# Latent attention heads: the squares for the norms of q and k move from ACT, tile by tile, to POOL, half of the tokens at once

## The chip, the cores and the metric

The kernel runs on one core of a Trainium2 chip. Its engines are PE (TensorE: matrix products and transposes), DVE (VectorE), ACT (ScalarE), POOL (GpSimd), and SP (SyncE), which issues the DMA transfers here. The metric is the device time of one execution in microseconds (us); lower is better.

## The reference, cut to what matters

Two decoder layers on 1024 tokens of width 1024. Layer 0 mixes tokens by stick-breaking attention, layer 1 by latent attention; each layer also has memory heads, an output projection and a SwiGLU. The change touches only this part of layer 1:

```
q  = (rms(c_q,  mla_q_norm)  @ w_q_up ).reshape(b, s, 12, 96)
kv = (rms(c_kv, mla_kv_norm) @ w_kv_up).reshape(b, s, 12, 64 + 64)
k  = concat(kv[..., :64], k_rope for every head)
v  = kv[..., 64:]
q, k = rms(q, g_qn), rms(k, g_kn)          # over the 96 columns of each head
q, k = rope on the last 32 columns of each
o = causal softmax attention(q, k, v)
```

The norms need the sum of squares of each token's 96 columns of q, and of the 64 columns of k of each head, to which the sum over the 32 shared columns (k_ss) is added.

## The kernel before

Every large product is made in three passes (high by high, high by low, low by high) of operands that are split into a rounded high half and the rest, the low half. `latent_heads` handles the 12 heads in 6 pairs. Per pair, `prepare` runs these steps on all engines, each engine taking its part of a step in its own queue:

- project n (n = 0 to 7, one for each tile of 128 tokens): PE makes q, k and v of two heads in PSUM bank 7; ACT copies them out to q32, k32 and v32 (the eviction) and squares q and k head by head, with the row sums as accumulator output. The next project waits for the eviction, the bank being only one.
- sum n (n = 0, 1: the half of the tokens): DVE adds k_ss. root n: ACT takes the square root, which needs another table of functions than the exponential. normalise n: DVE takes the reciprocal and multiplies q and k. rotate n: DVE and POOL share the rotary part; POOL first writes the rotated part of k.
- next weights: ACT rounds the weights of the pair after, POOL subtracts (lower_weights). values n: the split of v for head n, by ACT and then POOL (lower_values).
- turn n (n = 0 to 7): PE transposes 512 tokens of q or k of one head into bank 7, ACT writes the high half, scaled, DVE the low half (L2255). Turn n waits for the low half of turn n-1; turns 0 and 2 wait for the normalised and rotated halves.

The attention itself is the class `Attend`: four jobs for each pair (two heads, two halves of the queries, with 4 and 8 blocks of keys), 24 places in all. Its step kinds: S, scores of a tile by PE, and their row maximum by DVE (L934); P, the exponential by ACT (L909); I and R, the reciprocal of the row sum and the scaling of the row by DVE (L940, L946); T, transposes of a block of weights by PE (L885), then high half by ACT (L917) and low half by DVE (L951); V, the product with the values (PV, L894 and L896), which needs both halves; E, the end of a job, by ACT (L923) and DVE (L957). All jobs use one output bank, so the first V of a job waits for E of the job before. At place tau PE does T of tau, V of tau-1, then the scores that `plan` allows, then what `extras` lists for that place. Every engine walks the same list in order, so whatever stands in front in a queue delays the rest.

The first pair is prepared alone (the start-up, list PREPARE). Then a loop runs five rounds: the attention of pair g with the preparation of pair g+1 at the places that `extras` names. The last pair's attention runs with no preparation. POOL walks its own order: rotate 0, lower_weights, rotate 1, lower_values. SP stores outputs and loads the weights of the pair after next. Before the change these lines hold the places:

```
extras = {..., 4: ["project 4", "sum 0", "root 0"], 5: ["project 5", "normalise 0"], 6: ["project 6", "rotate 0"],
          7: ["project 7"], 8: ["next weights", "sum 1", "root 1"], 9: ["normalise 1"],
          10: ["rotate 1", "turn 0"], 11: ["used 1", "turn 1"], 12: ["turn 2"], 13: ["values 0", "turn 3"],
          14: ["turn 4"], 16: ["turn 5"], 18: ["turn 6"], 21: ["turn 7"]}
```

## Time and profile before

| | |
|---|---|
| median of 3 runs | 3078.08 us |
| lowest and highest | 3076.92 and 3081.86 us |
| span of the profiled execution, first to last instruction | 3078.6 us |
| mean granted TensorE clock over the span | 0.939 |

The profile gives the execution's span and no time of its own beside it; the span lies 0.5 us above the median. Busy shares are means over stages with different limits. The latent heads take the stretch from about 1765 to 2262 us: the start-up until about 1826, five rounds of some 75 us, and the last. A number in square brackets at the end of a timeline row is the time for which the engine stood idle before that instruction, with what released it.

### The profile page before, as it was taken

How to read it: one execution, taken by the hardware profiler on the slowest of the kernel's cores; microseconds unless marked ns; L12 is line 12 of the kernel's file. 1: busy time of each engine (PE TensorE's matmuls, PEld its weight loads, DVE VectorE, ACT ScalarE, POOL GpSimd, SP SyncE). 2: the span in 40 equal slices, each digit the busy share in tenths (PEclk: the TensorE clock that was granted, in tenths of full speed). 3: DMA queues.
4: the chain of work that ended last, by engine and by line, in shares of the span. 5: the costliest groups of instructions: out<-in, count | busy, mean ns of one | idle time of the engine just before them, and what ended most of it. 6: DMA issues, size and time to landing. Idle time of an engine off the chain costs nothing. (4 is left out here: it accounts for less than half of the span.)

```text
span 3078.6 us, 40579 instructions
## 1 busy us (share of the span) xinstructions
PE 2705.0 (88%) x13104; PEld 2209.8 (72%) x13104; DVE 1480.0 (48%) x2547; ACT 1295.7 (42%) x2794; POOL 1038.7 (34%) x722
## 2 busy tenths in 40 slices
PE   5679999878999998998668668888879899998999
PEld 4567777657788887887548657777757688887887
DVE  5636666744755553111562236666643755553111
ACT  4436566634333332222442246666633433332222
POOL 2035555530544443443102011111120544443443
PEclk9899999989999999999788879999989999999999
DMA  3021000041222223454102000000041222223454
GB/s 111 11 65 28 28 27 27 7 171 69 82 82 82 82 82 144 143 171 147 39 14 57 23 12 18 19 18 18 9 169 69 82 82 82 82 82 134 143 171 140
DMA packets 143097, 232.38 MB, mean 75 GB/s; under 512 B 17056, under 2 KB 93856, under 8 KB 143008
## 3 DMA queue, kind: packets, MB, share of 16 engines
q1 hardware_dynamic: 143008, 231.24, 22.7%
q8 instruction: 50, 0.82, 0.1%
q14 instruction: 39, 0.32, 0.0%
HBM read 182.98 MB, written 48.23 MB: 75 GB/s over the span
## 5 line engine op out<-in xcount | busy, mean ns | idle before, releaser
L1487 POOL TENSOR_TENSOR l0s_run_lo<-l0s_run,l0s_run_hi 128x512 fp32r<-128x512 f32 (+3 forms) x144 | 177.2, 1231 | 200.9 <-DVE l0s_run_hi L1653 200.9
L365 POOL TENSOR_TENSOR l0f_dn_lo<-l0f_dn_raw,l0f_dn_hi 128x1024 fp32r<-128x1024 f32 x44 | 106.0, 2411 | 138.9 <-ACT l0f_dn_hi L431 138.9
L365 POOL TENSOR_TENSOR l1f_dn_lo<-l1f_dn_raw,l1f_dn_hi 128x1024 fp32r<-128x1024 f32 x44 | 106.0, 2412 | 138.3 <-ACT l1f_dn_hi L431 138.3
L82 PE MATMUL banks<-l0f_dn_hi,l0f_a_hi 128*128 128x512 f32 x352 | 139.4, 396 | 8.9 <-issue 5.3
L82 PE MATMUL banks<-l1f_dn_hi,l1f_a_hi 128*128 128x512 f32 x352 | 138.6, 394 | 9.5 <-issue 5.3
L82 PE MATMUL banks<-l1f_T_hi,l1f_op_hi 128*128 128x512 f32 x352 | 139.3, 396 | 7.4 <-DVE l1f_T_lo L538 7.2
L82 PE MATMUL banks<-l0f_T_hi,l0f_op_hi 128*128 128x512 f32 x352 | 140.1, 398 | 6.1 <-DVE l0f_T_lo L538 5.9
L84 PE MATMUL banks<-l0f_T_hi,l0f_op_lo 128*128 128x512 f32 x352 | 139.0, 395 | 0.0
L83 PE MATMUL banks<-l0f_dn_lo,l0f_a_hi 128*128 128x512 f32 x352 | 138.9, 395 | 0.0
L84 PE MATMUL banks<-l0f_dn_hi,l0f_a_lo 128*128 128x512 f32 x352 | 138.8, 394 | 0.0
L84 PE MATMUL banks<-l1f_T_hi,l1f_op_lo 128*128 128x512 f32 x352 | 138.8, 394 | 0.0
L83 PE MATMUL banks<-l0f_T_lo,l0f_op_hi 128*128 128x512 f32 x352 | 138.8, 394 | 0.0
L83 PE MATMUL banks<-l1f_dn_lo,l1f_a_hi 128*128 128x512 f32 x352 | 138.6, 394 | 0.0
L84 PE MATMUL banks<-l1f_dn_hi,l1f_a_lo 128*128 128x512 f32 x352 | 138.6, 394 | 0.0
L83 PE MATMUL banks<-l1f_T_lo,l1f_op_hi 128*128 128x512 f32 x352 | 138.4, 393 | 0.0
L1643 DVE SCALAR_TENSOR_TENSOR l0s_run<-banks,l0s_soft 128x512 f32<-128x512 f32 (+3 forms) x144 | 80.2, 557 | 119.0 <-ACT l0s_soft L1545 117.6
L951 DVE TENSOR_TENSOR l1aa_pt_lo<-banks,l1aa_pt_hi 128x512 fp32r<-128x512 f32 (+2 forms) x144 | 79.3, 551 | 115.9 <-ACT l1aa_pt_hi L917 115.7
L592 DVE TENSOR_TENSOR l0f_a_lo<-l0f_a_raw,l0f_a_hi 128x512 fp32r<-128x512 f32 x44 | 33.2, 756 | 206.0 <-ACT l0f_a_hi L429 206.0
L592 DVE TENSOR_TENSOR l1f_a_lo<-l1f_a_raw,l1f_a_hi 128x512 fp32r<-128x512 f32 x44 | 33.2, 756 | 205.4 <-ACT l1f_a_hi L429 205.4
L82 PE MATMUL banks<-ht_hi,l0s_w_hi 128*128 128x512 f32 x288 | 119.4, 415 | 12.5 <-POOL l0s_w_lo L1477 12.5
L1516 ACT ACTIVATE l0s_soft<-banks 128x512 f32<-128x512 f32 (+3 forms) x144 | 71.0, 493 | 139.3 <-PE banks L1710 96.5
L360 POOL TENSOR_TENSOR l0f_hid<-l0f_c,l0f_gate 128x512 f32<-128x512 f32 x44 | 67.2, 1529 | 174.2 <-DVE l0f_c L553 174.2
(480 smaller groups left out, 8572.1 us busy)
## 6 DMA issues: line engine op xcount, KB each, us to landing
l0f_raw<-in_w_ffn_gu_dram SPq DMA_DIRECT2D x22, 1024.0 KB, 5.2
l0f_dn_raw<-in_w_ffn_down_dram SPq DMA_DIRECT2D x44, 512.0 KB, 3.9
l1f_raw<-in_w_ffn_gu_dram SPq DMA_DIRECT2D x22, 1024.0 KB, 5.1
l1f_dn_raw<-in_w_ffn_down_dram SPq DMA_DIRECT2D x44, 512.0 KB, 3.9
hidden_rows<-l0f_hid SPq DMA_DIRECT2D x22, 512.0 KB, 2.7
l0f_a_raw<-hidden_rows SPq DMA_DIRECT2D x44, 256.0 KB, 3.1
hidden_rows<-l1f_hid SPq DMA_DIRECT2D x22, 512.0 KB, 2.7
l1f_a_raw<-hidden_rows SPq DMA_DIRECT2D x44, 256.0 KB, 3.0
```

Source lines behind the costliest of these rows:

```text
L82: pe.matmul(out, l_hi, r_hi, start=first, stop=False, skip_group_check=True)
L83: pe.matmul(out, l_hi, r_lo, start=False, stop=False, skip_group_check=True)
L84: return pe.matmul(out, l_lo, r_hi, start=False, stop=last, skip_group_check=True)
L360: pool.tensor_tensor(hidden(q), cs[q][:], gate[q][:], ALU.mult).then_inc(hid_done, 1)
L365: pool.tensor_tensor(dn_lo[e][:], dn_raw[e][:], as_f32(dn_hi[e][:]), ALU.subtract).then_inc(dn_lo_done, 1)
L592: dve.tensor_tensor(a_lo[e][:], a_raw[e][:], as_f32(a_hi[e][:]), ALU.subtract).then_inc(a_lo_done, 1)
L951: dve.tensor_tensor(self.pt_lo[tau % 2][:, c0:HALF], self.t_ps[tau % 2][:, c0:HALF], as_f32(self.pt_hi[tau % 2][:, c0:HALF]), ALU.subtract ...
L1487: pool.tensor_tensor(run_lo[t % NR][:, f:HALF], run[t % NR][:, f:HALF], as_f32(run_hi[t % NR][:, f:HALF]), ALU.subtract).then_inc(run_spli ...
L1516: act.activation(s[:, f:HALF], psum[b % NZ][:, f:HALF], ACT.Abs).then_inc(abs_done, 1)
L1643: dve.scalar_tensor_tensor(r[:, f:HALF], psum[t % NZ][:, f:HALF], 0.0, soft[t % NA][:, f:HALF], ALU.max, ALU.add).then_inc(sp_done, 1)
```

## The change

ACT no longer squares in `project`. POOL gets a step squares(n, g) that multiplies all of q of half n by itself (128x768) into a buffer sq, waits until DVE has summed that, and does the same for k (128x512). DVE's sum n becomes two steps: sumq n sums q's squares; sumk n sums k's squares and adds k_ss. POOL's order becomes squares 0, rotate 0, squares 1, rotate 1, lower_weights, lower_values. sq lies over the buffers ra to rd of the rotation, which is why squares(1) waits for q_rot. In the loop, the sums, roots, normalisations and rotations stand one to three places later than before, turns 2 to 6 one place later (turn 4 from 14 to 15, turn 7 stays), and the scores of the next pair from place 13 on up to one place later.

```diff
--- before.py
+++ after.py
@@ -2030,8 +2030,9 @@
     wq = {n: mem(f"{tag}_wq_{n}", [P, NQ, QW], F32 if n == "raw" else F32R) for n in ("raw", "hi", "lo")}
     wk = {n: mem(f"{tag}_wk_{n}", [P, NK, KW], F32 if n == "raw" else F32R) for n in ("raw", "hi", "lo")}
     q32, k32 = mem(f"{tag}_q32", [P, G, QK]), mem(f"{tag}_k32", [P, G, QK])
-    junk = mem(f"{tag}_junk", [P, 2, QK + NOPE])
+    turned_at = mem.at
     ra, rb, rc, rd = (mem(f"{tag}_{n}", [P, G, H]) for n in ("ra", "rb", "rc", "rd"))
+    sq = Memory(nc, turned_at, mem.at)(f"{tag}_sq", [P, G // 2, QK])
     qt = {n: mem(f"{tag}_qt_{n}", [QK, 2, S], F32R) for n in ("hi", "lo")}
     kt = {n: mem(f"{tag}_kt_{n}", [QK, 2, S], F32R) for n in ("hi", "lo")}
     ss, std, rstd = (mem(f"{tag}_{n}", [P, 2, G]) for n in ("ss", "std", "rstd"))
@@ -2042,18 +2043,18 @@
 
     turns = [(a, h, half) for h in range(2) for half in range(2) for a in range(2)]
 
-    PREPARE = (["project 0", "project 1", "project 2", "project 3", "sum 0", "root 0", "normalise 0", "rotate 0",
-                "project 4", "project 5", "project 6", "project 7", "next weights", "sum 1", "root 1", "normalise 1",
+    PREPARE = (["project 0", "project 1", "project 2", "project 3", "sumq 0", "sumk 0", "root 0", "normalise 0", "rotate 0",
+                "project 4", "project 5", "project 6", "project 7", "next weights", "sumq 1", "sumk 1", "root 1", "normalise 1",
                 "rotate 1", "values 0"] + [f"turn {n}" for n in range(8)])
 
 
     extras = {0: ["values 1", "project 0"], 1: ["project 1"], 2: ["project 2"], 3: ["project 3"],
-              4: ["project 4", "sum 0", "root 0"], 5: ["project 5", "normalise 0"], 6: ["project 6", "rotate 0"],
-              7: ["project 7"], 8: ["next weights", "sum 1", "root 1"], 9: ["normalise 1"],
-              10: ["rotate 1", "turn 0"], 11: ["used 1", "turn 1"], 12: ["turn 2"], 13: ["values 0", "turn 3"],
-              14: ["turn 4"], 16: ["turn 5"], 18: ["turn 6"], 21: ["turn 7"]}
-
-    plan = [8, 9, 10, 11, 12, 13, 13, 14, 14, 15, 15, 16, 16, 16, 17, 18, 19, 20, 20, 21, 21, 22, 22, 23, 24]
+              4: ["project 4"], 5: ["project 5", "sumq 0"], 6: ["project 6", "sumk 0", "root 0"],
+              7: ["project 7", "normalise 0"], 8: ["next weights", "rotate 0"], 9: ["sumq 1"],
+              10: ["sumk 1", "root 1", "turn 0"], 11: ["used 1", "normalise 1", "rotate 1", "turn 1"],
+              13: ["values 0", "turn 2"], 14: ["turn 3"], 15: ["turn 4"], 17: ["turn 5"], 19: ["turn 6"], 21: ["turn 7"]}
+
+    plan = [8, 9, 10, 11, 12, 13, 13, 14, 14, 15, 15, 16, 16, 16, 16, 17, 18, 19, 20, 20, 21, 22, 22, 23, 24]
     OWN = ("values 1", "used 1")
     group = lambda n: slice(G // 2 * n, G // 2 * (n + 1))
     tiles = lambda n: slice(NS // 2 * n, NS // 2 * (n + 1))
@@ -2072,10 +2073,10 @@
                      lambda h, half, g: ot_dram[bass.ds(g * P + h * HD, HD), half * HALF:(half + 1) * HALF],
                      low, 4, psum["pair"], (6,), plan, extras)
         sem = lambda n: ctx.semaphore(f"{tag}_{n}")
-        (g_in, wq_in, wk_in, wq_hi, wk_hi, wq_lo, wk_lo, made, evicted, squared, v_hi, v_split, sums, root, inverse,
+        (g_in, wq_in, wk_in, wq_hi, wk_hi, wq_lo, wk_lo, made, evicted, squared, v_hi, v_split, sums, q_sums, k_sums, root, inverse,
          q_norm, k_norm, k_rope_done, rot_dve, rot_pool, q_rot, turned, t_hi, t_split, ones, scaled) = (
             sem(n) for n in ("g_in", "wq_in", "wk_in", "wq_hi", "wk_hi", "wq_lo", "wk_lo", "made", "evicted", "squared", "v_hi",
-                             "v_split", "sums", "root", "inverse", "q_norm", "k_norm", "k_rope_done",
+                             "v_split", "sums", "q_sums", "k_sums", "root", "inverse", "q_norm", "k_norm", "k_rope_done",
                              "rot_dve", "rot_pool", "q_rot", "turned", "t_hi", "t_split", "ones", "scaled"))
         block = ctx.enter_context(nc.Block())
         bank = psum[7]
@@ -2092,7 +2093,7 @@
                 sp.dma_start(wk["raw"][:], k_rows[:, :, bass.ds(g * KW, KW)]).then_inc(wk_in, 16)
 
             at_.begin(sp)
-            for s in (made, evicted, squared, v_split, turned, t_split):
+            for s in (made, evicted, v_split, turned, t_split):
                 sp.sem_inc(s, 1)
             load(0)
             sp.wait_ge(ones, 1)
@@ -2126,6 +2127,16 @@
                     pool.wait_ge(hi, g + 1)
                     pool.tensor_tensor(w["lo"][:], w["raw"][:], as_f32(w["hi"][:]), ALU.subtract).then_inc(lo, 1)
 
+            def squares(n, g, first=False):
+                e = 2 * g + n
+                if not first:
+                    pool.wait_ge(q_rot, 2 * e)
+                pool.wait_ge(evicted, 1 + NS * g + NS // 2 * (n + 1))
+                pool.tensor_tensor(sq[:], q32[:, group(n), :], q32[:, group(n), :], ALU.mult).then_inc(squared, 1)
+                pool.wait_ge(q_sums, e + 1)
+                pool.tensor_tensor(sq[:, :, 0:NOPE], k32[:, group(n), 0:NOPE], k32[:, group(n), 0:NOPE],
+                                   ALU.mult).then_inc(squared, 1)
+
             def rotate(n, g):
                 e, x1n, x2n = 2 * g + n, x1[:, tiles(n)], x2[:, tiles(n)]
                 pool.wait_ge(inverse, e + 1)
@@ -2140,14 +2151,16 @@
                 pool.wait_ge(rot_dve, 2 * e + 2)
                 pool.tensor_tensor(x2n, four(rc, n), four(rd, n), ALU.add).then_inc(q_rot, 1)
 
-            def prepare(g):
+            def prepare(g, first=False):
+                squares(0, g, first)
                 rotate(0, g)
+                squares(1, g)
+                rotate(1, g)
                 lower_weights(g + 1)
-                rotate(1, g)
                 lower_values(0, 2 * g)
 
             lower_weights(0)
-            prepare(0)
+            prepare(0, True)
             with pool.Fori(0, PAIRS - 1) as g:
                 lower_values(1, 2 * g + 1)
                 prepare(g + 1)
@@ -2177,13 +2190,6 @@
                     act.activation(q32[:, two, :], bank[:, 0:QW].rearrange("p (g d) -> p g d", d=QK), ACT.Copy)
                     act.activation(k32[:, two, 0:NOPE], kv[:, :, 0:NOPE], ACT.Copy)
                     act.activation(v32[:, two, :], kv[:, :, NOPE:], ACT.Copy).then_inc(evicted, 1)
-                    act.wait_ge(evicted, 1 + NS * g + n + 1)
-                    act.wait_ge(squared, 1 + NS * g + n)
-                    for h in range(2):
-                        one = slice(2 * n + h, 2 * n + h + 1)
-                        act.activation(junk[:, h, 0:QK], q32[:, 2 * n + h, :], ACT.Square, accum_out=ss[:, 0, one])
-                        last = act.activation(junk[:, h, QK:], k32[:, 2 * n + h, 0:NOPE], ACT.Square, accum_out=ss[:, 1, one])
-                    last.then_inc(squared, 1)
                 elif what == "root":
                     act.wait_ge(sums, 2 * g + n + 1)
                     act.activation(std[:, :, group(n)], ss[:, :, group(n)], ACT.Sqrt, bias=k["eps"][:, 0:1],
@@ -2227,8 +2233,13 @@
 
                 what, n = step.split()[0], int(step[-1]) if step[-1].isdigit() else 0
                 e = 2 * g + n
-                if what == "sum":
-                    dve.wait_ge(squared, 1 + NS * g + NS // 2 * (n + 1))
+                if what == "sumq":
+                    dve.wait_ge(squared, 2 * e + 1)
+                    dve.tensor_reduce(ss[:, 0, group(n)], sq[:], AX, ALU.add).then_inc(q_sums, 1)
+                elif what == "sumk":
+                    dve.wait_ge(squared, 2 * e + 2)
+                    dve.tensor_reduce(ss[:, 1, group(n)], sq[:, :, 0:NOPE], AX, ALU.add).then_inc(k_sums, 1)
+                    dve.wait_ge(k_sums, e + 1)
                     ks = ss[:, 1, group(n)].rearrange("p (t h) -> p t h", h=2)
                     dve.tensor_tensor(ks, ks, k_ss[:, tiles(n)].unsqueeze(2).broadcast_to([P, NS // 2, 2]),
                                       ALU.add).then_inc(sums, 1)
```

## Rows read from the trace of the kernel before

**Rows 1.** page, part 1: busy us, share of the span, instructions

```profile
PE 2705.0 (88%) x13104; PEld 2209.8 (72%) x13104; DVE 1480.0 (48%) x2547; ACT 1295.7 (42%) x2794; POOL 1038.7 (34%) x722
```

**Rows 2.** windows of the third and fourth round: busy us by engine, PEclk granted clock

```profile
2014.00:2090.00 76.00, 65.39 (x433) 58.65 (x432) 47.58 (x98) 51.99 (x167) 13.60 (x12) 0.91 0.07 18
2090.00:2164.00 74.00, 62.52 (x434) 55.43 (x432) 47.51 (x98) 52.01 (x167) 13.69 (x12) 0.98 0.08 19
```

**Rows 3.** waits of the phase: us in total, times, longest

```profile
PE banks L894 <- DVE l1aa_pt_lo L951: 44.0, 46, 3.4
```

**Rows 4.** timeline of PE, third round: start us, us, instruction, [idle before]

```profile
2018.05 0.50 PE L894 MATMUL banks<-l1aa_pt_hi,l1a_v 128*128 128x512 f32 x1 [0.56 <-DVE l1aa_pt_lo L951]
...
2034.27 0.69 PE L894 MATMUL banks<-l1aa_pt_hi,l1a_v 128*128 128x384 f32 x1 [3.40 <-DVE l1aa_pt_lo L951]
...
2040.74 0.62 PE L2298 MATMUL banks<-ident,l1a_k 128*96 128x128 f32 x4 [1.36 <-DVE l1a_qt_lo L2255]
...
2044.55 0.78 PE L894 MATMUL banks<-l1aa_pt_hi,l1a_v 128*128 128x512 f32 x1
```

**Rows 5.** timeline of ACT, third round

```profile
2014.05 0.28 ACT L2184 ACTIVATE l1a_junk<-l1a_q 128x96 f32<-128x96 f32 x1
...
2015.18 1.28 ACT L2189 ACT_TABLE_LOAD   x1
...
2030.74 1.28 ACT L2189 ACT_TABLE_LOAD   x1
...
2032.94 0.31 ACT L2189 ACTIVATE l1a_std<-l1a_ss,eps 128x16 f32<-128x16 f32 x1 [0.92 <-DVE l1a_ss L2233]
...
2033.64 1.28 ACT L909 ACT_TABLE_LOAD   x1
...
2034.94 1.01 ACT L909 ACTIVATE l1aa_p<-banks,l1aa_nmx 128x896 f32<-128x896 f32 x1
```

**Rows 6.** timeline of DVE, third round

```profile
2013.75 0.16 DVE L2233 TENSOR_TENSOR l1a_ss<-l1a_ss,k_ss 128x8 f32<-128x8 f32 x1
...
2017.91 0.24 DVE L2237 RECIPROCAL l1a_rstd<-l1a_std 128x16 f32<-128x16 f32 x1
...
2020.10 0.15 DVE L940 RECIPROCAL l1aa_rinv<-l1aa_rsum 128x1 f32<-128x1 f32 x1
...
2031.24 1.67 DVE L2233 TENSOR_TENSOR l1a_ss<-l1a_ss,k_ss 128x8 f32<-128x8 f32 x1
```

**Rows 7.** timeline of POOL, third round

```profile
2030.27 2.61 POOL L2127 TENSOR_TENSOR l1a_wq_lo<-l1a_wq_raw,l1a_wq_hi 128x1152 fp32r<-128x1152 f32 x1 [5.59 <-ACT l1a_wq_hi L2161]
...
2034.46 1.39 POOL L2132 TENSOR_TENSOR l1a_k<-k_rot,l1a_rstd 128x256 f32<-128x256 f32 x1 [0.35 <-DVE l1a_rstd L2237]
...
2036.67 0.45 POOL L2138 TENSOR_TENSOR l1a_rd<-l1a_q,rope_tab 128x128 f32<-128x128 f32 x1
```

**Rows 8.** groups by form, POOL, 1630 to 1760 us: xcount, busy us, mean ns

```profile
L1843 POOL TENSOR_TENSOR l1i_wq_lo<-l1i_wq_raw,l1i_wq_hi 128x768 fp32r<-128x768 f32 x8 | 14.7, 1838 | 8.7 <-ACT l1i_wq_hi L1930 8.7
```

**Rows 9.** groups by form, DVE, 1500 to 1560 us

```profile
L1188 DVE TENSOR_REDUCE l1m_hss<-l1m_q_sq 128x16 f32<-128x1024 f32 x2 | 2.4, 1220 | 13.3 <-ACT l1m_q_sq L1113 13.3
...
L1233 DVE TENSOR_REDUCE l1m_hss<-l1m_k_sq 128x8 f32<-128x512 f32 x1 | 0.7, 686 | 0.0
```

**Rows 10.** timeline of PE, fourth round

```profile
2094.08 0.50 PE L894 MATMUL banks<-l1aa_pt_hi,l1a_v 128*128 128x512 f32 x1 [0.56 <-DVE l1aa_pt_lo L951]
...
2119.77 0.50 PE L894 MATMUL banks<-l1aa_pt_hi,l1a_v 128*128 128x512 f32 x1
```

**Rows 11.** timeline of the start-up, ACT, DVE and PE

```profile
1783.84 0.31 ACT L2189 ACTIVATE l1a_std<-l1a_ss,eps 128x16 f32<-128x16 f32 x1 [0.23 <-DVE l1a_ss L2233]
...
1785.53 0.33 ACT L2177 ACTIVATE l1a_q<-banks 128x192 f32<-128x192 f32 x1 [1.38 <-PE banks L84]
...
1800.66 2.47 DVE L2239 TENSOR_TENSOR l1a_q<-l1a_q,l1a_rstd 128x768 f32<-128x768 f32 x1
...
1807.60 1.09 PE L2298 MATMUL banks<-ident,l1a_k 128*96 128x128 f32 x4 [9.48 <-DVE l1a_qt_lo L2255]
```

## The prediction

> **What bounds the kernel now.** I began with the page's busy shares. PE is busy 88% of the span [rows 1], so a change on other engines counts only where PE waits for them. Only the attention phase of the latent layer is touched: a start-up that prepares the first pair of heads with nothing else to run, five full rounds in which one pair's attention runs while the next is prepared, and a last round that prepares nothing. The second view was the windows of two of these rounds: the third took 76 us with 65.39 us of PE work at a granted clock of 0.91, the fourth 74 us with 62.52 us at 0.98 [rows 2]. Third came the list of waits. PE's largest is for the low half of the transposed weights (L951), 44.0 us over the phase in 46 waits [rows 3]. Fourth, the timeline of the third round shows where these lie. PE runs nearly without a break through places 0 to 7, waits 0.56 us at place 6, then stands still 3.40 us at place 10, and 1.36 us before turn 1 [rows 4].
>
> The 3.40 us has this cause. At place 8 ACT rounds the next weights and loads the table for the square root at 2030.74, but the root runs only at 2032.94, because it waits 0.92 us for DVE [rows 5]. DVE's addition of k_ss takes 1.67 us there, against 0.16 us for the same instruction at place 4 [rows 6]. POOL's subtraction of 2.61 us began at 2030.27, and the addition ended when that ended [rows 7]. So a DVE operation with two SBUF operands stands still while a POOL operation runs. The high half that PE needs sits behind the root in ACT's queue.
>
> **What is removed.** Per tile ACT loses four squarings, each with its read of the accumulator. They began at 2014.05 and the next instruction at 2015.18 [rows 5], so the four take 1.1 us: 8.8 us a round with eight tiles. PE hardly gains by this. Between two projects it has transposes, PV and scores to do, and the bank is emptied in that time; only the wait of 0.56 us comes from ACT's place-4 root. I count 0.7 us for it and the small one behind it, gained a round.
>
> **What is added.** POOL squares 128x768 and 128x512 for each half. It has no squaring now. The nearest row of 768 columns with two operands took 1.84 us [rows 8]; by the same slope 512 would be 1.25 us, and as k's squares are read with gaps I take 1.35 us. Bounds: 1.5 to 2.3 us and 1.1 to 2.0 us. DVE sums them: 512 columns took 0.69 us and 1024 took 1.22 us [rows 9], so 768 cost 0.95 us, and both 1.65 us a half. A round thus gives DVE 3.3 us and POOL 6.4 us, both of which are far from full; what counts is the order.
>
> The Trainium skill's GPSIMD Engine Reference (4.1, Engine selection) says that a two-input elementwise operation is about twice as slow there as on VectorE and belongs on the latter. By a DVE multiplication the q square would be an estimated 0.9 us and the chain below about 1 us shorter; the row of 1.84 us is what I use.
>
> **The middle of a round, step by step** (times of the third round). Root 0 moves to place 6. Two table loads at 1.30 us, root and high half 0.8 us and the exponential 0.9 us make 4.3 us at ACT; put behind project 6, whose eviction ends at 2023.1, that makes the last eviction start at 2027.45 and place 8's high half end at 2028.6. With no root at place 8, ACT has place 9's high half at 2030.8. DVE is later: normalise 0, 2.2 us from its reciprocal (2017.91) to the next operation (2020.10) [rows 6], now stands at place 7 and ends at 2028.0; then low half, row scaling and maximum until 2030.7, rotate 0 until 2031.25, low half until 2031.8. PE's PV comes at 2031.8 instead of 2034.27: 2.4 us earlier.
>
> The chain of half 1 now begins there. POOL ends its rotation at 2031.6, squares q until 2033.45; DVE sums until 2034.4. POOL squares k until 2035.85. DVE does a low half and then wants to scale a row, an operation that I let wait for POOL as the addition did: until 2036.45. Maximum over 1024 columns 1.15, sum and k_ss 0.85: 2038.45. Root 0.3, high half of q^T 0.6, low half 0.7: PE starts turn 1 at 2040.1, not 2040.74 [rows 4]. Nearly all of the 2.4 us is gone: PE has nothing to do from about 2035.5, a pause of 4.5 us.
>
> Then comes what used to be done earlier. ACT must reload the exponential's table (1.28 us, the next operation 1.30 us after its start [rows 5]) and do the 1024-column exponential (896 columns took 1.01 us), 1.2 us with its accumulator, before the high half of k^T, ready at 2042.7. DVE has normalise 1 (2.2 us) and rotate 1 ahead of the low half. Its reciprocal ends at 2040.6; POOL's three products follow it, with 2.7 us from the first's start (2034.46) to the last's end (2037.12) [rows 7], and rotate 1 ends at about 2043.5. Low half until 2044.2, that of place 12 until 2044.85, the output's sum until 2045.5. Only one output bank exists, so PE starts PV of the third job at 2045.55; before it was 2044.55 [rows 4], and in the fourth round, whose clock was high, 2119.77, which is 2043.74 in this round's time (76.03 us lie between the two PVs at place 6) [rows 4, 10]. That is 1.0 to 1.8 us late, 1.4 taken. Turn 2 is still to come then. It and turns 3 and 4 are spaced by their round trip of some 2.4 us, and PV at place 17 waits behind turn 4, but two short waits at places 18 and 20 become one: 0.5 us more. PE now pauses over 4 us twice in place of 3.4 us once. The rounds of rows 2 differ by 2 us for 0.07 of clock; I add 0.4 us. Sum: 2.3 us a round, 11.5 us in five.
>
> The Trainium skill's ScalarE: Activation LUTs (What ACT_TABLE_LOAD costs) counts about 2.66 us for each change of set, with a drain. By that the k^T step would be some 0.6 us later, an estimated 3 us in all. The row of 1.28 us, with the next operation directly behind, disagrees, and the sum goes by the row.
>
> **The start-up.** Root 0 stands in ACT's queue ahead of the eviction of project 4. It ran at 1783.84 [rows 11], after squares of 1.1 us and a sum of 0.2 us, so the fourth eviction ended at 1782.45. Now 1.85+0.95+1.35+0.85 us and the semaphores stand between: the root runs at 1787.6 and the eviction at 1788.0, not 1785.53 [rows 11]: 2.5 us later. After project 7 the same chain takes some 5.4 us, where squares, weights and root took 2.6 us. In return lower_weights goes behind rotate 1, so normalise 1's q part takes 0.96 and not 2.47 us [rows 11], and the k part behind it is free of POOL's subtraction too. Turn 1 starts at about 1809.5 against 1807.60 [rows 11]: 1.9 us lost.
>
> POOL's later weights are needed only in the next round; the DMA of the weights after those stands in SP's queue behind the round's stores anyway; lower_values 0 has ten places. Each costs nothing, and would cost its own 2 to 4 us if PE reached the next round first. The last round changes only in the place of two row scalings: nothing.
>
> The profile's span is 3078.6 us, 0.5 above the median of 3078.08; I add to the latter: 3078.1 + 1.9 + 11.5 = **3091.5 us**.
>
> **Rivals.** (a) The gain stays. If sums and root 1 end before PE is through with place 10, PE keeps the 2.4 us and most of the slow clock goes. It decides once turn 1 starts before about 2038, 2 us less chain than I count: 3078.1 + 1.9 - 5x(2.4+0.7) gives 3064.5. For it: ACT is relieved by 8.8 us and the 3.40 us wait disappears. Against: everything of half 1 is two places later. Chance 0.2. (b) Waits move and cancel, only the start-up remains: 3078 to 3084, chance 0.2. It needs the exponential's table load and normalise 1 to hide behind PE's work at places 11 and 12. (c) Port waits on both sides and a clock low from place 10 to 16 every round: POOL at its upper bounds, 1.2 us a half on the chain, 2 us of clock, 5 us a round in all: 3105, chance 0.1. (d) Forecast, 3085 to 3098: 0.5.
>
> A measurement of this kernel tells about 0.2%, 6 us. (d) and (c) are slower; of (b) nine tenths are within it; (a) is faster. Faster 0.2, same 0.18, slower 0.62. From 3066 to 3104 leaves out parts of (a) and (c), 2 in 10. The likeliest case's own range is 3085 to 3098.
>
> **What would show it.** POOL's squares near 1.8 and 1.35 us; DVE's row scaling at place 10 longer than 0.62 us beside POOL's k square; no wait of 3.4 us at place 10, but one of 4 us before turn 1 and one before PV at place 13; rounds of about 77.6 us. Wrong would be turn 1 before 2038 in this round's time, or PV of the third job earlier than before. Then my order of DVE's queue at places 10 to 12 was priced too high.

## The result, and the profile after

| | before | after |
|---|---|---|
| median, 9 runs each | 3081.2 us | 3089.14 us |
| lowest and highest | 3076.92 and 3083.32 | 3087.25 and 3099.04 |
| span of the profiled execution | 3078.6 | 3086.6 |

The ratio of the two kernels over all their runs is 1.0032, with a 95% interval of 1.0023 to 1.004: some 10 us slower, between 7 and 12. The two medians of the table are 7.9 us apart. The forecast was 3091.5 us, 13.4 us over the median of before as it stood then.

The page of the kernel after, part 1. ACT has lost 53 us of work against [rows 1]; DVE has gained 13 and POOL 26; PE's share has not moved.

```profile
PE 2704.6 (88%) x13104; PEld 2211.4 (72%) x13104; DVE 1493.2 (48%) x2571; ACT 1242.5 (40%) x2410; POOL 1065.0 (35%) x746
```

The windows of its third and fourth round, to be read beside [rows 2]: 77.5 and 77.1 us where there were 76 and 74, and a granted clock of 0.91 and 0.89.

```profile
1992.40:2069.90 77.50, 64.34 (x435) 57.62 (x434) 50.17 (x103) 43.15 (x102) 17.92 (x16) 0.91 0.07 18
2069.90:2147.00 77.10, 65.33 (x435) 58.47 (x435) 50.23 (x103) 43.15 (x102) 17.93 (x16) 0.89 0.07 18
```

PE's waits in the phase, in us in total, their number and the longest. The one for the weights' low half is down from 44.0 us [rows 3] to 28.6, but the one before the turns has grown, and a wait for o_out, the sum at the end of a job, has come up. First two lines of the kernel before, then those of the kernel after:

```profile
PE banks L2298 <- DVE l1a_qt_lo L2255: 21.0, 9, 9.5
PE banks L894 <- DVE l1aa_o_out L957: 3.4, 3, 2.2
...
PE banks L2309 <- DVE l1a_qt_lo L2266: 29.5, 9, 8.5
PE banks L894 <- DVE l1aa_pt_lo L951: 28.6, 37, 3.2
PE banks L894 <- DVE l1aa_o_out L957: 21.1, 13, 2.8
```

PE's timeline in the fourth round, which begins with project 0 at 2069.89. From here on, a time "in the round" is counted from that instruction of the round in question.

```profile
2069.89 0.30 PE L82 MATMUL banks<-l1a_wq_hi,cq_hi 128*128 128x192 f32 x1
...
2105.51 0.50 PE L894 MATMUL banks<-l1aa_pt_hi,l1a_v 128*128 128x512 f32 x1 [0.67 <-DVE l1aa_pt_lo L951]
...
2108.16 0.69 PE L894 MATMUL banks<-l1aa_pt_hi,l1a_v 128*128 128x384 f32 x1 [1.71 <-DVE l1aa_pt_lo L951]
2108.65 0.52 PE L896 MATMUL banks<-l1aa_pt_lo,l1a_v 128*128 128x384 f32 x1
2108.97 0.63 PE L82 MATMUL banks<-l1a_kt_hi,l1a_qt_hi 96*128 96x512 f32 x1
2109.39 0.63 PE L83 MATMUL banks<-l1a_kt_lo,l1a_qt_hi 96*128 96x512 f32 x1
...
2115.86 1.06 PE L2309 MATMUL banks<-ident,l1a_k 128*96 128x128 f32 x4 [2.54 <-DVE l1a_qt_lo L2266]
...
2121.31 0.79 PE L894 MATMUL banks<-l1aa_pt_hi,l1a_v 128*128 128x512 f32 x1 [2.56 <-DVE l1aa_o_out L957]
```

The 3.40 us of [rows 4] at place 10 have become 0.67 and 1.71 us. In their stead PE waits 2.54 us before turn 1 and 2.56 us before the third job's first PV. Turn 1 is at 45.97 in the round and this PV at 51.42; before, in the third round (begun at 1993.18), they were at 47.56 and 51.37 [rows 4]. So turn 1 comes 1.6 us earlier, the PV at the same time, and the round is longer behind it. The pause before turn 1 is not the same in each round: 2.5 us in the first and fourth, 3.5 and 4.4 us in the second and third. How long PE stands there depends on how fast it was before (see e11), and turn 1 itself comes at 45.6 to 46.0 in all four.

DVE of the same round, around the squares. The sum of q's squares waits 1.51 us for POOL. The row scaling at 2110.87 takes 1.23 us beside POOL's square of k. From 2115.84 the queue is solid: normalise 1, rotate 1, low half of k^T, the output's sum at 2120.59, for which PE waits.

```profile
2107.34 0.29 DVE L2261 TENSOR_TENSOR l1a_q<-l1a_ra,l1a_rb 128x128 f32<-128x128 f32 x1
2107.55 0.55 DVE L951 TENSOR_TENSOR l1aa_pt_lo<-banks,l1aa_pt_hi 128x384 fp32r<-128x384 f32 x1
2109.61 0.95 DVE L2238 TENSOR_REDUCE l1a_ss<-l1a_sq 128x8 f32<-128x768 f32 x1 [1.51 <-POOL l1a_sq L2135]
...
2110.87 1.23 DVE L946 TENSOR_SCALAR l1aa_p<-l1aa_p,l1aa_rinv 128x768 f32<-128x768 f32 x1
2112.02 1.21 DVE L934 TENSOR_REDUCE l1aa_nmx<-banks 128x1 f32<-128x1024 f32 x1
...
2115.84 0.24 DVE L2248 RECIPROCAL l1a_rstd<-l1a_std 128x16 f32<-128x16 f32 x1
...
2120.59 0.67 DVE L957 TENSOR_TENSOR l1aa_o_out<-banks,l1aa_o_tmp 64x512 f32<-64x512 f32 x1
```

POOL and then ACT in the same round. ACT has its table loaded early and waits 4.44 us for the sums; behind root 1 it must load the exponential's table and do the exponential before k^T's high half.

```profile
2107.45 0.49 POOL L2152 TENSOR_TENSOR l1a_q<-l1a_rc,l1a_rd 128x128 f32<-128x128 f32 x1 [2.44 <-DVE l1a_rb L2258]
2108.11 1.47 POOL L2135 TENSOR_TENSOR l1a_sq<-l1a_q 128x768 f32<-128x768 f32 x1 [0.16 <-POOL l1a_q L2152]
2110.64 1.04 POOL L2137 TENSOR_TENSOR l1a_sq<-l1a_k 128x512 f32<-128x512 f32 x1 [1.07 <-DVE l1a_ss L2238]
```

```profile
2114.06 0.31 ACT L2195 ACTIVATE l1a_std<-l1a_ss,eps 128x16 f32<-128x16 f32 x1 [4.44 <-DVE l1a_ss L2244]
...
2115.11 1.28 ACT L909 ACT_TABLE_LOAD   x1
2116.41 1.11 ACT L909 ACTIVATE l1aa_p<-banks,l1aa_nmx 128x1024 f32<-128x1024 f32 x1
...
2117.51 0.67 ACT L2203 ACTIVATE l1a_kt_hi<-banks,l1a_gcol 96x512 fp32r<-96x512 f32 x1
```

The start-up, ACT and then PE, beside [rows 11]. It begins at 1761.68 (before: 1765.80), so the root moved from 18.0 to 21.8 us behind its beginning, and turn 1 from 41.8 to 43.1.

```profile
1783.43 0.31 ACT L2195 ACTIVATE l1a_std<-l1a_ss,eps 128x16 f32<-128x16 f32 x1 [4.60 <-DVE l1a_ss L2244]
1783.65 0.31 ACT L2190 ACTIVATE l1a_q<-banks 128x192 f32<-128x192 f32 x1
```

```profile
1804.75 1.09 PE L2309 MATMUL banks<-ident,l1a_k 128*96 128x128 f32 x4 [8.54 <-DVE l1a_qt_lo L2266]
```

Rounds one to four, from project 0 to the next project 0, took 76.79, 75.34, 76.02 and 74.02 us before (mean 75.54) and 76.72, 77.51, 77.47 and 77.06 after (mean 77.19): 1.65 us each. The start-up, from its first project to the first round, took 75.25 us before and 76.51 after. Five rounds and these 1.3 us make 9.5 us; the ratio says 10.

### The profile page after: what moved, and what is told of

Its sections match the earlier page's. It is cut to its first block and busy times, and to the rows that moved or that the text cites. A ratio compares the mean times of both kernels' runs of the same rounds, so it can differ in the third digit from the quotient of the medians.

```text
span 3086.6 us, 40220 instructions
## 1 busy us (share of the span) xinstructions
PE 2704.6 (88%) x13104; PEld 2211.4 (72%) x13104; DVE 1493.2 (48%) x2571; ACT 1242.5 (40%) x2410; POOL 1065.0 (35%) x746
## 5 line engine op out<-in xcount | busy, mean ns | idle before, releaser
L360 POOL TENSOR_TENSOR l1f_hid<-l1f_c,l1f_gate 128x512 f32<-128x512 f32 x44 | 67.2, 1528 | 172.8 <-DVE l1f_c L553 172.8
```

Of the source, the lines that this page charges most:

```text
L360: pool.tensor_tensor(hidden(q), cs[q][:], gate[q][:], ALU.mult).then_inc(hid_done, 1)
```

## The experiments

The change has six separable parts: who squares; POOL's order, with lower_weights behind rotate 1; the places of half 0's steps (normalise 0 from place 5 to 7 and so on); those of half 1's steps; the places of turns 2 to 6 with the plan of the scores; and the start-up. The table gives the means of rounds one to four, measured on PE's timeline of one profile of each kernel, in us: length, turn 1, the third job's first PV, and from that PV to the end of the round. The cuts of code are shortened where "..." stands.

| kernel | ratio to before (95%) | round | turn 1 | PV | rest |
|---|---|---|---|---|---|
| before | | 75.54 | 47.7 | 51.5 | 24.1 |
| after | 1.0032 (1.0023 to 1.004) | 77.19 | 45.9 | 51.3 | 25.9 |
| e1 places only | 1.0045 (1.0032 to 1.0058) | 78.60 | 47.3 | 52.7 | 25.9 |
| e2 squares only | 0.9990 (0.9981 to 0.9998) | 74.62 | 47.0 | 50.7 | 23.9 |
| e3 turn 0 first | 1.0031 (1.0019 to 1.0042) | 76.94 | 44.1 | 51.1 | 25.9 |
| e4 subtraction late | 0.9981 (0.9972 to 0.9990) | 74.74 | 46.8 | 50.7 | 24.0 |
| e5 start-up | 1.0029 (1.0018 to 1.0039) | 77.13 | 46.3 | 51.7 | 25.4 |
| e6 weights at 15 | 0.9994 (0.9985 to 1.0003) | 76.07 | 45.6 | 49.5 | 26.5 |
| e7 half 1 late only | 0.9983 (0.9975 to 0.9992) | 74.26 | 42.9 | 48.3 | 25.9 |
| e8 half 0 late only | 1.0051 (1.0038 to 1.0064) | 78.87 | 50.5 | 54.6 | 24.3 |
| e9 as e7, old turns | 0.9968 (0.9956 to 0.9980) | 73.17 | 42.9 | 48.8 | 24.4 |
| e10 after, old turns | 1.0007 (0.9998 to 1.0016) | 76.05 | 45.9 | 51.7 | 24.4 |
| e11 square ahead | 1.0035 (1.0022 to 1.0048) | 77.28 | 46.0 | 51.5 | 25.8 |
| e12 as e9, start-up | 0.9968 (0.9957 to 0.9980) | 73.59 | 43.3 | 49.1 | 24.5 |

**e1, places only.** The kernel before with the new places, plan and POOL order; ACT squares as before.

```diff
-              4: ["project 4", "sum 0", "root 0"], 5: ["project 5", "normalise 0"], 6: ["project 6", "rotate 0"],
-              7: ["project 7"], 8: ["next weights", "sum 1", "root 1"], 9: ["normalise 1"],
+              4: ["project 4"], 5: ["project 5"], 6: ["project 6", "sum 0", "root 0"],
+              7: ["project 7", "normalise 0"], 8: ["next weights", "rotate 0"],
+              10: ["sum 1", "root 1", "turn 0"], 11: ["used 1", "normalise 1", "rotate 1", "turn 1"], ...
```

> The changed places (extras and plan) and POOL's changed order, but the squares stay with ACT, tile by tile, and sum n stays one step. My theory is that the loss comes from half 1's chain being put at places 9 to 11, in front of PE's next work, and only partly from POOL's and DVE's squares themselves. Without the squares on that chain DVE has no wait of 1.5 us and no sum of 0.95 us at place 9, no k sum of 0.7 us and no stalled row scaling at place 10, so root 1 comes some 3 us earlier than in the changed kernel: rounds of 75 to 76 us against 77.3, the pause before turn 1 down to 1 to 2 us, the time within 4 us of before (ratio 0.998 to 1.002). The rival, that the places do all the harm: rounds of 77 us, ratio 1.003.

The theory missed; the rival held, and the harm is more than it said. The rounds are 3.1 us longer than before and 1.4 us longer than in the changed kernel. The places cost; at the new places, to let POOL square gives part of it back.

**e2, squares only.** The changed kernel with the old places, turns and plan; sumq, sumk and root of a half stand at one place. POOL's new order stays in it, so against before it has two parts, and against e4 below only the squares.

```diff
+              4: ["project 4", "sumq 0", "sumk 0", "root 0"], 5: ["project 5", "normalise 0"], 6: ["project 6", "rotate 0"],
+              7: ["project 7"], 8: ["next weights", "sumq 1", "sumk 1", "root 1"], 9: ["normalise 1"], ...
```

> The squares by POOL with DVE's two sums, at the old places and with the old plan. The chain of POOL and DVE from the last eviction of a half to the root is 1.47+0.95+1.04+0.7+0.2 us and semaphores, 4.7 us, where ACT's squares took 1.1 us. At place 4 it now holds ACT for some 3 us more, at place 8 about as long as POOL's subtraction held k_ss before. I expect a wait at place 6 of over 2 us (0.56 us before) and one at place 10 like that of before, rounds of 77 to 79 us, ratio 1.003 to 1.006: the old places are no cure. The rival, that the late places alone cost the time: rounds of 75 us or less, ratio at most 1.001.

This missed too, and its rival held. The rounds are 0.9 us shorter than before, and not 2 to 3 us longer. PE's wait at place 10 grows to 4.65 us, but the small waits at places 6 and 9 (0.56 and 0.60) are gone, and it ends no later in the round (40.6 against 41.1).

**e3, turn 0 first.** In the changed kernel, place 10 lists turn 0 ahead of sumk 1 and root 1.

```diff
-              10: ["sumk 1", "root 1", "turn 0"], ...
+              10: ["turn 0", "sumk 1", "root 1"], ...
```

> The changed kernel with turn 0 put before sumk 1 and root 1 at place 10. My theory says that the pause before turn 1 is turn 0 waiting behind root 1 in ACT's queue, and that the time is set one step later, by the output's sum behind normalise 1, rotate 1 and the two low halves in DVE's queue. So the pause before turn 1 shrinks from 2.5 to 4.4 us to about 1.5 us, but PV of the third job starts no earlier (0 to 0.7 us later), with the pause before it grown: rounds of 77 to 78 us, the time that of the changed kernel within 3 us. The rival, that turn 1's wait is what costs the time: rounds 2 to 3 us shorter, ratio to before about 1.000.

This came as expected. Turn 1 comes 1.8 us earlier (44.1) and the PV of the third job only 0.2. Its wait for o_out is 4.00 us in the fourth round, where it was 2.56. What turn 1 gains is given back one step later: normalise 1 and rotate 1 are still in DVE's queue ahead of the output's sum.

**e4, the subtraction late.** The kernel before, with POOL's lower_weights behind rotate 1.

```diff
                 rotate(0, g)
-                lower_weights(g + 1)
                 rotate(1, g)
+                lower_weights(g + 1)
```

> The kernel before, with one thing of the change alone: POOL's lower_weights behind rotate 1 instead of before it. The k_ss addition at place 8 no longer meets POOL's subtraction of 2.6 us: it takes 0.16 us instead of 1.67 us, and root 1 and the high half behind it come 0.9 us earlier (ACT's wait of 0.92 us goes, the table load then bounds). In the start-up normalise 1's q part takes 0.96 us, not 2.47 us, and turn 1 starts about 3 us earlier. The PE pause at place 10 falls from 3.4 to 2.5 us, rounds get 0.9 us shorter or more if the slow clock shortens: 3 to 10 us faster in all, ratio 0.997 to 0.999. If the long addition had another cause, nothing changes.

The rounds came as expected. DVE's addition of k_ss at place 8, which took 1.67 us beside POOL's subtraction [rows 6], takes 0.15, and PE's wait at place 10 falls from 3.4 to 2.49 us: rounds 0.8 us shorter, the time 5.9 us. This is nearly the whole gain of e2, whose rounds are 0.1 us shorter than e4's; so at the old places the squares on POOL are worth nothing in the rounds. In the start-up they cost: e2's, from the first project to the first round, took 78.61 us and e4's 75.03, and the ratios to before, 0.9990 and 0.9981, leave e2 some 3 us slower, with intervals that overlap. Turn 1 of e4's start-up came only 0.2 us earlier in this trace and not 3; on this see the start-up further below. DVE and then PE of the kernel with the late subtraction, fourth round:

```profile
2102.39 0.15 DVE L2233 TENSOR_TENSOR l1a_ss<-l1a_ss,k_ss 128x8 f32<-128x8 f32 x1
```

```profile
2104.51 0.69 PE L894 MATMUL banks<-l1aa_pt_hi,l1a_v 128*128 128x384 f32 x1 [2.49 <-DVE l1aa_pt_lo L951]
```

**e5, start-up.** The changed kernel with project 4 ahead of sumq 0 in PREPARE.

```diff
-    PREPARE = ([..., "project 3", "sumq 0", "sumk 0", "root 0", "normalise 0", "rotate 0", "project 4", "project 5",
+    PREPARE = ([..., "project 3", "project 4", "sumq 0", "sumk 0", "root 0", "normalise 0", "rotate 0", "project 5",
```

> The changed kernel with project 4 put before sumq 0, sumk 0 and root 0 in the start-up list alone. The wait of 2.48 us before project 5, which is the eviction of project 4 behind root 0, falls to 0.76 us like those of its neighbours; from the first project to turn 1 it is 41.3 us instead of 43.07 us at a like clock, and nothing changes in the rounds (77.3 us). The time falls by 1.7 us, less than a measurement tells. If the start-up's loss lies in the last chain of squares alone, the wait goes but turn 1 comes no earlier.

The start-up came as expected, the rounds did not. Turn 1 of the start-up is at 41.1 instead of 43.1 us, but the first round takes 78.39 us instead of 76.72, with 5 us more at the lower of TensorE's two clock levels before the third job's PV. The time is the same.

**e6, weights at 15.** e4, and the rounding of the next weights on ACT moved from place 8 to 15, with POOL's lower_values ahead of lower_weights.

```diff
-              8: ["next weights", "sum 1", "root 1"], ... 14: ["turn 4"], 16: ["turn 5"]
+              8: ["sum 1", "root 1"], ... 14: ["turn 4"], 15: ["next weights"], 16: ["turn 5"]
```

> The kernel before with POOL's lower_weights late (as in the run before of that kind) and next weights moved from place 8 to place 15; squares by ACT, old places otherwise. At place 8 the root then follows squares and sum at once: 1.8 us less of ACT in front of the high half that PE waits for. The pause at place 10 falls from 2.5 us to about 0.7 us, and the slow clock after it should mostly go. Rounds of 72 to 73.5 us against 75.3, 9 to 16 us faster than before, ratio 0.995 to 0.997. The rival, that a place-15 load of 1.8 us on ACT makes a new wait at places 16 to 18 of the same size: ratio about 0.998.

The expected rounds of 72 to 73.5 us did not come. The PV of the third job is at 49.5, 1.2 us earlier than in e4, but the rest takes 26.5 us instead of 24.0: the 1.85 us of rounding now stand in ACT's queue ahead of the end of a job, and a wait of 1.01 us for o_out appears there. The lower clock level also lasts longer in the rest, 5.6 us instead of 1.5 in the mean; how the 2.5 us divide was not tried.

**e7 and e8, one half late.** By then my theory was that half 1's chain, two places later, was what cost. e7 is the changed kernel with half 0's steps at their old places; e8 is the changed kernel with half 1's steps, the turns and the plan at their old ones.

```diff
-              4: ["project 4"], 5: ["project 5", "sumq 0"], 6: ["project 6", "sumk 0", "root 0"],
-              7: ["project 7", "normalise 0"], 8: ["next weights", "rotate 0"], 9: ["sumq 1"], ...
+              4: ["project 4", "sumq 0", "sumk 0", "root 0"], 5: ["project 5", "normalise 0"], 6: ["project 6", "rotate 0"],
+              7: ["project 7"], 8: ["next weights"], 9: ["sumq 1"], ...
```

> The changed kernel with half 0's sums, root, normalisation and rotation back at places 4, 5 and 6; half 1 stays late (places 9 to 11), as do turns and plan. Places alone cost 0.45% and squares alone nothing, so I now hold that the loss is half 1's late chain with the turns: root 1 and the exponential's table load, normalise 1 and rotate 1 stand in front of PV of the third job. Then this keeps the pauses before turn 1 and before that PV (2.5 us) and the rounds stay at 76.5 to 77.5 us, ratio 1.002 to 1.004. The rival, that half 0's move to places 5 to 8 is what costs: rounds of 75 us, ratio at most 1.001.

And for e8, with the turns of before behind it:

```diff
+              7: ["project 7", "normalise 0"], 8: ["next weights", "rotate 0", "sumq 1", "sumk 1", "root 1"], 9: ["normalise 1"],
+              10: ["rotate 1", "turn 0"], 11: ["used 1", "turn 1"], ...
```

> The counterpart: half 0 late (places 5 to 8) as in the changed kernel, but half 1, the turns and the plan at the old places. By my theory the pauses at places 11 and 13 go and one pause stays at place 10, of some 5 us, because the squares of half 1 now start behind rotate 0: rounds of 75 to 76 us, ratio 0.999 to 1.002. The rival, half 0's move as the cause: rounds of 77 us, ratio 1.003.

The theory fell. With half 0 back, half 1 may be late and the round is 1.3 us shorter than before; with only half 0 late it is 3.3 us longer, and PE stands still 7.5 us at place 10. PE in e7's fourth round (begun at 2062.32):

```profile
2097.38 0.47 PE L894 MATMUL banks<-l1aa_pt_hi,l1a_v 128*128 128x512 f32 x1
...
2099.21 0.45 PE L894 MATMUL banks<-l1aa_pt_hi,l1a_v 128*128 128x384 f32 x1 [0.91 <-DVE l1aa_pt_lo L951]
...
2099.67 0.39 PE L82 MATMUL banks<-l1a_kt_hi,l1a_qt_hi 96*128 96x512 f32 x1
2099.90 0.39 PE L83 MATMUL banks<-l1a_kt_lo,l1a_qt_hi 96*128 96x512 f32 x1
...
2105.32 0.61 PE L2309 MATMUL banks<-ident,l1a_k 128*96 128x128 f32 x4 [3.27 <-DVE l1a_qt_lo L2266]
...
2110.77 0.80 PE L894 MATMUL banks<-l1aa_pt_hi,l1a_v 128*128 128x512 f32 x1 [3.21 <-DVE l1aa_o_out L957]
```

Here the PVs of places 9 and 10 come at 35.06 and 36.89 in the round; in the changed kernel at 35.62 and 38.27, with waits of 0.67 and 1.71 us. Behind them the two score products begin 0.23 us apart in e7 and 0.42 in the changed kernel, whose clock had just fallen to its lower level; from the PV of place 10 to the next PV it takes 4.39 us against 2.36. DVE's sum of q's squares is at 36.76 in e7's round, with no wait, and at 39.72 in the changed kernel's: the 2.96 us by which turn 1 and the PV of the third job are late.

The slower scores are not what makes them late. In the third round of the changed kernel (begun at 1992.42) the clock kept its upper level until 43.7, so the same scores ran at full speed. PE only waits longer before turn 1, which comes at 45.93 as against 45.97, and the PV at 51.38 as against 51.42. DVE's maximum over these scores stands directly behind its row scaling in both rounds. PE, DVE and PE again, all of that third round:

```profile
2031.10 0.40 PE L82 MATMUL banks<-l1a_kt_hi,l1a_qt_hi 96*128 96x512 f32 x1
2031.33 0.40 PE L83 MATMUL banks<-l1a_kt_lo,l1a_qt_hi 96*128 96x512 f32 x1
...
2033.35 1.23 DVE L946 TENSOR_SCALAR l1aa_p<-l1aa_p,l1aa_rinv 128x768 f32<-128x768 f32 x1
2034.50 1.21 DVE L934 TENSOR_REDUCE l1aa_nmx<-banks 128x1 f32<-128x1024 f32 x1
...
2038.35 1.06 PE L2309 MATMUL banks<-ident,l1a_k 128*96 128x128 f32 x4 [4.35 <-DVE l1a_qt_lo L2266]
2043.80 0.79 PE L894 MATMUL banks<-l1aa_pt_hi,l1a_v 128*128 128x512 f32 x1 [2.55 <-DVE l1aa_o_out L957]
```

**e9 and e10, old turns.** e7 and the changed kernel, each with turns 2 to 6 and the plan as before the change.

```diff
-              13: ["values 0", "turn 2"], 14: ["turn 3"], 15: ["turn 4"], 17: ["turn 5"], 19: ["turn 6"], 21: ["turn 7"]}
+              12: ["turn 2"], 13: ["values 0", "turn 3"], 14: ["turn 4"], 16: ["turn 5"], 18: ["turn 6"], 21: ["turn 7"]}
-    plan = [..., 16, 16, 16, 16, 17, 18, 19, 20, 20, 21, 22, 22, 23, 24]
+    plan = [..., 16, 16, 16, 17, 18, 19, 20, 20, 21, 21, 22, 22, 23, 24]
```

Places 10 and 11 stay as they are in e7 and in the changed kernel.

> Half 0 of the norm's steps at the old places 4 to 6, half 1's three steps at the new places 9 to 11, turns and plan as in the kernel before. Theory A (the later turns 2 to 6 and the order of the PVs lengthen the last third of a round): turn 1 at 43 us of the round and the third job's PV at 48.3 as in the run with half 1 late, but the rest of the round 24.2 instead of 25.9; rounds of 72.5 against 74.3, the span 3065 to 3068 us. Theory B (the rest of the round is long because it takes back what was left undone before the third job's PV; where the turns stand is nothing to it): the rest stays at 25.5 to 26, rounds of 74, span 3073.

> The changed kernel with the turns' places and the order of the PVs as before; the steps of the norms of both halves stay at the later places. Theory A: the third job's PV where the changed kernel has it, at 51.3, and the rest 24.2 instead of 25.9: rounds of 75.5 against 77.2, span 3079 us. Theory B: turn 2 at place 12 waits and the rest stays near 25.7: rounds of 77, span 3086.

Theory A held, wherever the PV stands: the rest is 1.5 us shorter in both. The PV itself is 0.4 us later, so a round gains 1.1 us in each, somewhat less than was expected. The turns' places and the plan were moved together and not tried apart. Of e9, PE's waits of the phase and, from the fourth round (begun at 2063.32), turn 2 and the PV:

```profile
PE banks L2309 <- DVE l1a_kt_lo L2266: 19.6, 11, 3.3
...
PE banks L894 <- DVE l1aa_o_out L957: 3.4, 3, 2.2
```

```profile
2110.78 1.06 PE L2309 MATMUL banks<-ident,l1a_q 128*96 128x128 f32 x4 [2.51 <-DVE l1a_kt_lo L2266]
...
2112.14 0.78 PE L894 MATMUL banks<-l1aa_pt_hi,l1a_v 128*128 128x512 f32 x1
```

In e7 PE waits 3.21 us for o_out and has turn 2 still to come. In e9 turn 2 lies in this pause, the PV waits for nothing, and the turns behind have a lead of one. e9 is faster than both kernels of this case. The same places with the squares left on ACT were not tried.

**e11, square ahead.** The changed kernel with a memory of its own for sq (ss, std and rstd make room for it), and, in the loop, POOL's square of q for half 1 ahead of rotate 0.

```diff
                 squares(0, g, first)
-                rotate(0, g)
-                squares(1, g)
+                squares(1, g, parts="q")
+                rotate(0, g)
+                squares(1, g, parts="k")
```

> The changed kernel with a memory of its own for the squares, and POOL's square of q for half 1 ahead of rotate 0 (inside the loop), so that sumq 1 finds it done. If half 1's chain is late because the squares wait for rotate 0's last addition: no wait at sumq 1 (1.5 before), root about 1.5 us earlier, turn 1 at 44.3 instead of 45.9 and the third job's PV at 50 instead of 51.3; rounds of 76, span 3080. Rival: POOL's square now stands before rotate 0, which makes DVE's subtraction and with it sumq 1 as late as before: turn 1 at 45.9, rounds of 77.2, span 3086.

Nothing was gained in the time, as the rival said, though not by its reason. The wait at sumq 1 is gone, and the sum 1.1 us earlier in the round, but rotate 0 is later by POOL's square, and with it the low half of place 9: PE waits 2.18 us there instead of 1.71. DVE's maximum over 1024 columns then waits for the scores, which PE makes at the lower clock (fourth round):

```profile
2110.08 1.23 DVE L946 TENSOR_SCALAR l1aa_p<-l1aa_p,l1aa_rinv 128x768 f32<-128x768 f32 x1
2112.68 1.23 DVE L934 TENSOR_REDUCE l1aa_nmx<-banks 128x1 f32<-128x1024 f32 x1 [1.37 <-PE banks L2067]
```

So two chains lead to root 1: DVE's, with POOL's square in it, and PE's, with its waits and the scores. In the changed kernel DVE's is the longer one: in the fourth round, at the lower clock, the last score product began at 2111.53 and the maximum at 2112.02 without a wait, and in the third the scores were done almost 2 us before it. In e11 PE's is the longer one. In its third round, where the first two of the six products ran at the upper level, the maximum waits 0.60 us instead of 1.37, turn 1 is at 45.52 and the PV at 50.97, 0.8 us earlier than in the fourth and 0.4 us earlier than in the changed kernel. To shorten one chain shows the other; a round of e11 with all six at the upper level was not seen.

**e12, e9 with the other start-up.** The start-up list of e5 in e9.

> The same as the kernel with half 0's steps at the old places, half 1's late and the old turns, and in the start-up project 4 ahead of sumq 0. As far as the start-up is a wait of its own: 1.5 to 2 us less than that kernel, span 3063 to 3066 with theory A, 3071 with B. Rival: the clock takes it back, as in the changed kernel with this start-up, whose time did not move: no difference.

The rival held: the start-up is 1.6 us shorter, the first round takes 74.51 us instead of 72.90 with 5 us more at the lower clock before that PV, and the time is that of e9 (3071.71 and 3072.24 us).

## Why the prediction was right, and where its sizes were off

**Direction and mechanism.** The 3.40 us at place 10 went, one pause came before turn 1 and one before the third job's PV, and the round became longer. The PV of place 10 was put 38.6 us into the round and came at 38.1 in the mean. Root 0 of the start-up was put at 21.8 us behind its beginning and came at 21.8. The direction, the pauses and the queues they come from were right; that the sum landed within 2.4 us of the median is in part luck, as two terms were off in opposite ways, and the part of the change that the forecast blamed is not the one that costs. The pauses were put at over 4 us each and were 2.5 to 4.4 and 2.6 to 2.8 us. One sign that was named for a wrong forecast, the third job's PV earlier than before, came in the mean (51.3 and 51.5), though not in the third round (51.38 and 51.37).

**The chain to turn 1, too long by a microsecond.** Forecast 46.9 in the round, measured 45.9. POOL's squares took 1.47 and 1.04 us, not 1.84 and 1.35; together 0.7 us. The remaining 0.4 us is about what the PV of place 10 came early (38.1 in the mean, not 38.6): the 0.7 us a round that the prediction counts for the waits at places 6 and 9 is not in its sum. The sums cost 0.95 and 0.67 as worked out. The stall of the row scaling beside POOL's square of k is real: 1.23 us at this place, where it took 0.83 before and 0.61 in e1, whose POOL does not square. The Trainium skill's SBUF — State Buffer (SBUF: two separate sides) says that GpSimd and some DVE operations exclude each other for the whole of an instruction; the trace agrees, with the scaling here, and with k_ss at 0.15 us in e4 against 1.67.

**The price on POOL.** For 768 columns of two operands POOL took 1.47 us and DVE (normalise) 0.96, a factor of 1.5. The GPSIMD Engine Reference of the Trainium skill (4.1, Engine selection) has about 2. The bounds for q's square were 1.5 to 2.3 us, so it came out at the cheap end. As to the decision, e4 and e2 show that the squares on POOL, by themselves, are no gain at the old places: 0.1 us a round, against a start-up that is longer. At the new places e1 and the changed kernel differ by 1.4 us a round in their favour.

**The PV of the third job, mis-sized.** This is the term that was most wrong: 1.4 us late was taken, and against the mean of before it is 0.2 us early (51.3 and 51.5). One microsecond comes from the chain above, the rest from before's other rounds: I took the third and the fourth, and the first, with 3.6 us at the lower clock at its beginning, was at 52.6.

**What comes behind it, mis-sized the other way.** 0.5 us for later turns and 0.4 for the clock were taken; the rest of a round grew by 1.8 us. e9 and e10 put 1.5 us of it on the turns' places and the plan. I had seen that turn 2 comes after the PV, but not that before the change it fills the pause, so that its move costs PE's own time too. PE before, third round, with the PV at 2044.55 behind it:

```profile
2043.19 1.06 PE L2298 MATMUL banks<-ident,l1a_q 128*96 128x128 f32 x4 [1.23 <-DVE l1a_kt_lo L2255]
```

The clock's part can be estimated. Behind that PV the third and fourth rounds of before spent 4.9 and 0 us at the lower level and took 24.65 and 23.45 us, so 1 us there costs about 0.25 us. In the mean of four rounds these stretches grew from 2.2 to 4.6 us: some 0.6 us, near the 0.4 that was taken, and partly contained in the 1.5. The sum, 1.65 us a round instead of 2.3, comes out near because the error here and that of the PV have opposite signs.

**The start-up.** 1.3 us in place of 1.9. It is the balance of two larger terms: in e1 and e6, where ACT squares and the weights are late, turn 1 of the start-up was at 38.8 and 39.0, against 41.8 before and 43.1 after. So the late weights gave back some 3 us and the squares took 4. One trace tells it only roughly, since in e4 and e2, with the same start-ups as e1 and after but 5 to 7 us more at the lower clock at their beginning, turn 1 was at 41.6 and 45.2. e5 and e12 show that a start-up shorter by 2 us does not show in the time, since the next round runs longer at the lower clock; the same may hold for a longer one, which was tried by itself only between e4 and e2, where some 3 us did show.

**What the forecast did not separate.** It blamed half 1's chain. Taking the parts one at a time (rounds, in us): POOL's order gives -0.8 (before to e4); the squares on POOL -0.1 (e4 to e2); half 1 later gives -1.5 (e2 to e9); half 0 later costs +2.9 (e9 to e10, and e7 to after); turns and plan cost +1.1 (e9 to e7, and e10 to after). Together +1.6. Half 0's price had been seen only as work that delays a PV. It comes in two steps. Normalise 0 and rotate 0 stand at places 7 and 8 in DVE's queue, so that the low half of place 10 begins at 37.66 in the changed kernel's fourth round and at 36.30 in e7's: 1.4 us. And DVE's sum then waits 1.51 us for POOL's square of q, which stands behind rotate 0. That these two make the whole price is read from the traces; e11, which takes the second away, gets nothing for it in three rounds and 0.4 us in one, because PE's chain then bounds. It is not the clock: behind the third job's PV the lower level lasted 4.4 us in e7 and 4.6 in the changed kernel, 3.6 in e9 and 3.1 in e10, and ahead of that PV the changed kernel's third round shows that the clock does not matter there. DVE of the changed kernel's fourth round, normalise 0:

```profile
2102.30 0.96 DVE L2250 TENSOR_TENSOR l1a_q<-l1a_q,l1a_rstd 128x768 f32<-128x768 f32 x1
2103.17 1.11 DVE L2252 TENSOR_TENSOR l1a_k<-l1a_k,l1a_rstd 128x512 f32<-128x512 f32 x1
...
2104.76 0.69 DVE L951 TENSOR_TENSOR l1aa_pt_lo<-banks,l1aa_pt_hi 128x512 fp32r<-128x512 f32 x1 [0.41 <-ACT l1aa_pt_hi L917]
```

From 2101.41 to the end of the next low half at 2108.10 this pause of 0.41 us is DVE's only one, and the two low halves in it are those for which PE waits 0.67 and 1.71 us. At places 5 and 6 the same steps cost nothing: in e7's fourth round PE has no wait over 0.5 us until that of 0.91. With half 1 at its old places half 0's delay costs still more, 4.3 us (e2 to e8), and with half 0 late half 1's delay gives back more, 2.8 us (e8 to e10), so the parts do not simply add.

**Left open.** The fifth and the last round together took 116.7 us before and 122.0 after, in one profile each, with 13.7 us more at the lower clock. Of the 5.3 us, 2.2 lie ahead of the last round's first PV and 3.0 behind it, where nothing was forecast: 37.8 us before, with 10.2 us at the lower level, and 40.9 after, with 19.7. e3 runs the same code there as after and took 39.1 us with 13.7, so the clock has a part in it; the rest was not tried. In the other stages, which the change does not touch, the two profiles differ by 5 us the other way.

## What to carry to other kernels

When several steps are moved at once, price each one by the queue that it lands in, and not only by the chain that it belongs to: here half 0 was the one that cost, though its result is needed only at place 10, since it was moved to where DVE was full. Even an order of one engine that looks like a side matter is a part: without e4, its 0.8 us would have been credited to the squares. A pause of the bounding engine is a place to put its own work: to move the turns out of it, with the plan, cost 1.1 us a round. And a shorter wait is worth its time only up to the next one; e3, e5, e6 and e12 each gained over a microsecond at one place and gave it back within a round.

## What the runs showed of the hardware

- TensorE's clock fell during or behind waits, but not at the same point each time. In the changed kernel's fourth round it fell to its lower level at 37.9, within the wait of 1.71 us that follows one of 0.67; in the third round, with the same two waits, only at 43.7, within the wait of 4.35. In e7's fourth round it fell at 43.7, 0.7 us behind the wait of 3.27, and stayed there for 10.2 us instead of 17.1. A lower level while PE waits for others anyway cost nothing (turn 1 at 45.93 and 45.97). A product of 512 columns starts 0.42 us behind the one before at the lower level, 0.23 at the upper.
- A table load took 1.28 us and the next operation began 1.30 us after its start in every case seen: no drain beyond that, as in [rows 5].
- A POOL product of an operand by itself took 1.47 us for 768 columns, where one with two different operands took 1.84 [rows 8]; whether the one operand is the reason was not tried.
- Stages that no kernel here changes differ from one execution to the next: the latent heads began between 1758.8 and 1768.2 us over these kernels. A difference of spans of some microseconds is therefore no measurement of an edit. The length of the rounds within one trace is a better one, though the four rounds of before spread from 74.0 to 76.8 us: five times the difference of the mean rounds and that of the start-ups came within 2 us of what each ratio of the table says.
